# Reordering the head of a one-core transformer step: features begun on half of k, and two groups of additions moved to GpSimd

## What is computed

```python
mod = silu(c) @ w_mod + b_mod                       # nine vectors of 1024: shift, scale, gate x 3
h = rmsnorm(x, ng[0]) * (1 + sc1) + sh1
x = x + g1 * 0.5 * (silu(h @ w_gate) * (h @ w_up)) @ w_down      # FFN 1, 1024 -> 2816 -> 1024
h = rmsnorm(x, ng[1]) * (1 + sc2) + sh2
...                                                  # attention group and recurrent group, w_out
x = x + g3 * 0.5 * swiglu(rmsnorm(x, ng[2]) * (1 + sc3) + sh3)   # FFN 2
y = rmsnorm(x, final_g)
```

## Time and profile before

| | us |
|---|---|
| median of three runs | 2238.14 |
| the profiled execution | 2237.18 |
| its span in the trace | 2235.4 |
| PE busy | 2161.9 (97%) |
| DVE busy | 1537.1 (69%) |
| ACT busy | 825.0 (37%) |
| POOL busy | 67.6 (3%) |

### The profile page before, as it was taken

The page is one execution under the profiler, slowest core; times in us unless marked ns, Lnnn a source line. Parts: engine busy times, 40 slices in busy tenths (PEclk is TensorE's granted clock), DMA queues, the critical chain, the costliest instruction groups (busy, mean ns, idle before and its releaser), DMA issues.

```text
span 2235.4 us, 34069 instructions
## 1 busy us (share of the span) xinstructions
PE 2161.9 (97%) x13144; PEld 2100.3 (94%) x13144; DVE 1537.1 (69%) x2543; ACT 825.0 (37%) x1503; POOL 67.6 (3%) x120
## 2 busy tenths in 40 slices
PE   5999999999999999999999999999999999999997
PEld 4989999999999999899988889899999999999996
DVE  6977777777878865766767874695555547756556
ACT  5632232234212133565257762453222323411122
POOL 0000000000000000000023130000000000000000
PEclk9999999999999999999999999999999999999999
DMA  7333323334534403001133211132121223521312
GB/s 294 134 106 121 120 96 136 105 123 141 179 127 157 145 19 150 30 29 48 38 84 110 55 41 38 61 112 89 59 84 63 75 72 113 179 94 59 114 31 85
DMA packets 86133, 219.03 MB, mean 98 GB/s; under 512 B 10624, under 2 KB 38144, under 8 KB 86016
## 3 DMA queue, kind: packets, MB, share of 16 engines
q1 hardware_dynamic: 82176, 208.52, 27.4%
q0 software_dynamic: 3840, 8.92, 1.8%
HBM read 172.56 MB, written 35.92 MB: 93 GB/s over the span
## 4 chain that ended last, share of the span: by engine, by line
PE 87%; DVE 6%; ACT 3%; DMA 2%; issue 1%; SPq 0%; DVEq 0%; POOL 0%; ACTq 0%
PE ps L818 15%; PE ps L819 15%; PE ps L820 15%; PE ps L893 9%; PE ps L895 9%; PE ps L894 9%; PE ps L1073 7%; PE ps L1204 2%; PE ps L1149 1%; PE ps L1055 1%; PE ps L1190 1%; PE ps L1157 1%; DMA sb_stage<-in_w_mod 1%; ACT sb_pr L1721 1%; DVE sb_nmx L2461 1%
## 5 line engine op out<-in xcount | busy, mean ns | idle before, releaser
L818 PE MATMUL ps<-sb_hH,sb_wH 128*128 128x384 f32 x1664 | 563.0, 338 | 9.5 <-DVE sb_hL L1915 4.7
L819 PE MATMUL ps<-sb_hL,sb_wH 128*128 128x384 f32 x1664 | 557.2, 335 | 0.0
L820 PE MATMUL ps<-sb_hH,sb_wL 128*128 128x384 f32 x1664 | 557.2, 335 | 0.0
L818 PEld LDWEIGHTS ps<-sb_hH,sb_wH 128*128 128x128 f32 x1664 | 313.1, 188 | 16.9 <-DVE sb_hL L1915 5.4
L819 PEld LDWEIGHTS ps<-sb_hL,sb_wH 128*128 128x128 f32 x1664 | 313.4, 188 | 1.2 <-issue 0.3
L820 PEld LDWEIGHTS ps<-sb_hH,sb_wL 128*128 128x128 f32 x1664 | 313.3, 188 | 0.0
L2225 DVE SCALAR_TENSOR_TENSOR sb_x<-ps,sb_mod,sb_x 128x384 f32<-128x384 f32 (+2 forms) x384 | 186.1, 514 | 172.2 <-PE ps L820 167.0
L893 PE MATMUL ps<-sb_hH,sb_wH 128*128 128x384 f32 x704 | 236.2, 336 | 5.1 <-DVE sb_tmp L2085 3.9
L894 PE MATMUL ps<-sb_hL,sb_wH 128*128 128x384 f32 x704 | 235.9, 335 | 0.0
L895 PE MATMUL ps<-sb_hH,sb_wL 128*128 128x384 f32 x704 | 235.7, 335 | 0.0
L1368 ACT ACTIVATE sb_wH<-sb_wide 128x512 fp32r<-128x512 f32 x176 | 110.9, 633 | 228.7 <-DVE sb_wide L1969 223.7
(11 more groups left out here) (259 smaller groups left out, 3799.7 us busy)
## 6 DMA issues: line engine op xcount, KB each, us to landing
sb_raw<-in_w_gate SPq DMA_DIRECT2D x56, 512.0 KB, 3.6
sb_raw<-in_w_up SPq DMA_DIRECT2D x56, 512.0 KB, 3.5
sb_raw<-in_w_mod SPq DMA_DIRECT2D x56, 512.0 KB, 3.6
hidden<-sb_tmp SPq DMA_DIRECT2D x132, 192.0 KB, 2.1
sb_hid_raw<-hidden SPq DMA_DIRECT2D x40, 576.0 KB, 6.4
sb_raw<-in_w_dn SPq DMA_DIRECT2D x80, 256.0 KB, 2.6
sb_stage<-in_w_mod SPq DMA_DIRECT2D x4, 2048.0 KB, 15.7
sb_raw<-in_w_in SPq DMA_DIRECT2D x16, 512.0 KB, 3.5
```

The source lines that it names most:

```text
L818: pe.matmul(o, wH, xH, start=begin, stop=False)
L819: pe.matmul(o, wH, xL, start=False, stop=False)
L820: return pe.matmul(o, wL, xH, start=False, stop=end)
```

## The change

Five things change, all but the last two in the first 100 us:

1. **Transfers.** Three small tensors instead of ten are issued ahead of the `w_mod` blocks; the other seven come behind the second block. Weights of feature index 0 come between the second and the third block, weights of index 1 and 2 ahead of x of chunks 1 and 2.
2. **TensorE's order.** Features 0 and 1 are no longer run whole after the fourth `w_mod` block, but in parts (`early_part`) of k, around and between the products of the third and fourth block. ScalarE's and VectorE's orders in the head are rewritten to match (`early_one` splits one A block alone). `stats` and `spread` of chunks 1 and 2 move to features 2 and 3.
3. **Sums of chunk 2.** The seven additions of the squares of chunk 2 go from VectorE to GpSimd (`last_square`).
4. **Front differences.** The four differences of each `op_front`, 16 instructions in each of the two FFNs, go from VectorE to GpSimd (`op_differences`); casts and low parts wait for the last GpSimd instruction that reads their tile (`OP_LAST_READ`).
5. **A series.** The 16 small steps (and five more) for softplus of the recurrent part move from the head into the FFN's down stage (`series_step`).

The diff, cut to its core:

```diff
+OP_LAST_READ = {B11: 1, T3: 2, T1: 3, B22: 3, T2: 4, B21: 4, T4: 4}
...
+        SMALLS = ((cin[:], "c"), (bmod[:], "bmod"), (ng[:], "ng"))
+        LATER_SMALLS = ((glam[:, 0], "glam"), (fg[:], "fg"), (convw[:], "convw"), (convb[:], "convb"),
+                        (gbias[:], "gbias"), (h0[:], "h0"), (subg[:], "subg"))
...
         def mod_bank(n):
-            return 6 if n % 2 else 7
+            return 2 if n % 2 else 7
+        def early_bank(z, w, u):
+            return (2, 7)[u] if (z, w) == (0, 2) else 3 + u + 2 * (w % 2)
...
-            for b in MOD_FIRST:
+            for b in MOD_FIRST[:2]:
+                stage_load(b)
+            for dst, name in LATER_SMALLS:
+                sp.dma_start(dst, a[name]).then_inc(gw_in, 16)
+            early_load(0, 0)
+            for b in MOD_FIRST[2:]:
+                stage_load(b)
+            early_load(0, 1)
+            early_load(0, 2)
             x_load(1)
-            load_one(0, 0, 1, MAIN + 1)
-            load_one(0, 1, 1, MAIN + 1)
             x_load(2)
+            early_load(0, 3)
...
+            def last_square(k):                      # GpSimd
+                s, buf = nrm[0], sum_buf(0, 2)
+                n = square_at(0, 2, k)
+                pool.wait_ge(s["sq"], n + 1)
+                if k > 1:
+                    pool.wait_ge(s["acc"], added_at(0, 2, k - 1))
+                pool.tensor_tensor(buf, buf if k > 1 else tmp[:, (n - 1) % 2], tmp[:, n % 2], ALU.add).then_inc(s["acc"], 1)
+            def op_differences(z, p):                # GpSimd; the same four leave op_front on VectorE
+                base = 16 * z + 4 * p
+                pool.wait_ge(front, base + 4)
+                pool.tensor_tensor(op_raw(T1, p), op_raw(T3, p), op_raw(B11, p), ALU.subtract).then_inc(front_pool, 1)
...
+            for k in range(1, KT):
+                last_square(k)
+            for p in range(KT // 2):
+                op_differences(0, p)
...
-                             {(1, 0, 2): (stats, 1), (1, 1, 0): (spread, 1), (1, 1, 6): (stats, 2), (2, 0, 6): (spread, 2)})
+                             {(2, 0, 2): (stats, 1), (2, 1, 0): (spread, 1), (2, 1, 5): (stats, 2), (3, 0, 3): (spread, 2)})
...
+            early_part(0, 0, (0, 1))                 # TensorE, after two of four mod_products
+            mod_products(2)
+            early_part(0, 1, (0, 1))
+            for u in range(2):
+                early_part(0, u, (2, 3))
+            mod_products(3)
+            early_part(1, 0, range(4))
+            for k in (4, 5):
+                for u in range(2):
+                    early_part(0, u, (k,))
+            early_part(1, 1, range(4))
+            for k in (6, 7):
+                for u in range(2):
+                    early_part(0, u, (k,))
+            for u in range(2):
+                early_part(1, u, range(4, KT))
...
-            h_hi(0, 0, range(4))                     # ScalarE
-            early_cast(0, 0, 0)
+            h_hi(0, 0, (0,))
+            early_one(0, 0, A11)
+            h_hi(0, 0, (1,))
+            early_one(0, 0, A21)
...
+            squares(0, 2, x_in, range(3))
             root_copy(0, 1)
+            squares(0, 2, x_in, range(3, KT))
+            silu_first(0, 1, early_bank(0, 1, 0))
+            early_cast(0, 0, 3)
+            early_cast(0, 1, 3)
+            load_root()
             root_of(0, 2)
```

More of the change, by code:

```diff
@@ L810, in _ @@
                     sub_norm(c, hd)
+            for p in range(KT // 2):
+                op_differences(1, p)
         @blk.tensor
@@ L864, in _, with first_chunk @@
             stats(0, 0)
-            pe.wait_ge(c_ready, 1)
-            pe.wait_ge(smalls, N_SMALL)
+            pe.wait_ge(cons, 4)
             mod_products(0)
             spread(0, 0)
[L869 to L875, removed]
+            mod_products(1)
+            def first_chunk(z, u, n, w, between=None, index=0, ks=range(KT)):
+                bank = early_bank(z, index, u)
+                for k in ks:
                     o = ((A11, A12), (A21, A22))[u][k // 4]
@@ L965, in hooks @@
                     return between
-                for w in range(EARLY):
+                for w in range(0 if z else 2, EARLY):
                     for u in range(2):
-                        first_chunk(z, u, w + 1, FT * z + w - 1 if w > 1 else FT * z if z else None, hooks(w, u), w)
+                        first_chunk(z, u, w + 1, FT * z + w - 1 if w > 2 - z else FT * z if z else None, hooks(w, u), w)
                 feature(z, 0, 0, True, 28 * z)
@@ L1512, in ffn_act @@
             def ffn_act(z):
-                for w in range(0 if z else 1, EARLY):
-                    silu_first(z, FT * z + w, 3 + 2 * (w % 2))
+                for w in range(0 if z else 2, EARLY):
+                    silu_first(z, FT * z + w, early_bank(z, w, 0))
                     if w + 2 <= EARLY:
@@ L2305, in _, with low_at_tile @@
             scale_of(0, 0, 4)
-            apply(0, 0, None, range(0, 4))
-            dve.wait_ge(rl_exp, 1)
-            link(dve.tensor_scalar(q, y, 2.0, None, ALU.add))
-            link(dve.reciprocal(q, q))
-            link(dve.tensor_tensor(y, y, q, ALU.mult))
-            link(dve.tensor_tensor(q, y, y, ALU.mult))
-            link(dve.memset(r, 1.0 / 17))
-            for n in range(15, 0, -2):
-                link(dve.tensor_tensor(r, r, q, ALU.mult))
-                link(dve.tensor_scalar(r, r, 1.0 / n, None, ALU.add))
+            def low_at_tile(n, at):
+                return lambda k: early_one(0, n, at[k]) if k in at else None
+            apply(0, 0, low_at_tile(0, {1: A11, 2: A21}), range(0, 4))
             mod_add(2)
+            early_one(0, 0, A12)
+            early_one(0, 0, A22)
             mod_add(3)
@@ L2319, in _ @@
             scale_of(0, 4, KT)
-            shift_step(0)
-            early_low(0, 0, 0)
-            apply(0, 0, None, range(4, 6))
-            early_low(0, 1, 0)
-            apply(0, 0, None, range(6, KT))
-            early_low(0, 0, 1)
-            for k in range(1, KT):
-                sum_square(0, 1, k)
-            early_low(0, 1, 1)
-            inverse_of(0, 1)
-            for k in range(1, KT):
-                sum_square(0, 2, k)
-            early_low(0, 0, 2)
+            apply(0, 0, low_at_tile(1, {4: A11, 6: A21}), range(4, KT))
+            early_one(0, 1, A12)
+            early_one(0, 1, A22)
+            for k in range(1, 4):
+                sum_square(0, 1, k)
+            early_low(0, 0, 2)
+            for k in range(4, KT):
+                sum_square(0, 1, k)
+            early_low(0, 1, 2)
+            inverse_of(0, 1)
+            hid_first(0, 0)
+            shift_step(0)
+            hid_first(0, 1, early_bank(0, 1, 1))
+            early_low(0, 0, 3)
+            early_low(0, 1, 3)
             inverse_of(0, 2)
-            early_low(0, 1, 2)
             ffn_dve(0)
```

105 lines of the change are left out of this document (66 added, 39 removed).

## The result

| | before | after |
|---|---|---|
| median, six runs each | 2238.16 us | 2247.63 us |
| lowest to highest | 2234.83 to 2239.04 | 2245.70 to 2248.77 |
| span in the trace | 2235.4 us | 2243.9 us |

The ratio is 1.0045, with a 95% interval of 1.0034 to 1.0055: the changed kernel is slower by about 9.5 us. The prediction was 2236.1 us, its range ended at 2241.5, and "slower" had a chance of 0.13. It was wrong.

What follows compares the result with a forecast made beforehand. TensorE (PE), busy 2161.9 of 2235.4 us, was taken as the bound. 1.0 us from the head and 1.0 from the front differences made 2.0 us less, 2238.14 to 2236.1; range 2230.5 to 2241.5.

Steps and rivals of the forecast that it cites:

- The transfers and the start of the features: Head: blocks 1 and 3 land 1.4 us later, yet features 0 and 1 end 6.7 to 8.1 us earlier.
- GpSimd's additions: Sums of chunk 2: seven additions at 1.10 us each, spaced 1.22, ending at 66.0 instead of 62.0 us on VectorE.
- second case: TensorE behind its wait for `stats` 2: a slow stretch brings it to 71.1 us instead of 69.7.
- The second FFN: GpSimd's 19 us of differences lie beside four features of 8.3 us there: no effect on time.
- Gain left: 1.0 us: Head, at `spread` 2: it ends at 71.05 us, where TensorE reached the same matmul at 72.1 before; 1.0 us won.
- Front differences: First FFN: VectorE relieved of 8 us, GpSimd's 19 us just covered, 1.0 us won; lower end nothing.
- The wait at 111 us: TensorE's wait of 1.27 us at 111.53: gone or halved, 1.0 us of it won.
- GpSimd and VectorE hold each other: Rival, front differences: VectorE stands 17.6 us for GpSimd's 16 against 8 relieved, giving 2246 us; chance 0.11.
- its sign of being wrong: Sign for the blocking rival: VectorE's multiplications between 70 and 90 us much over 0.6 us apart.

Runs made afterwards that it cites:

- e6: Kernel before with only SP's order changed, stores of hidden tiles behind the weight loads: 2244.96 us (before 2238.36), ratio 1.0031.
- e1: Changed kernel with the front differences of both FFNs back on VectorE: 2248.11 us (before 2237.89), ratio 1.0041.
- e3: Changed kernel with stores ahead of loads in SP's queue and front differences back on VectorE: 2241.49 us (before 2237.89), ratio 1.0015.
- e8: e4 with VectorE's four front groups of the first FFN one feature later: 2238.98 us (before 2238.36), ratio 1.0005.
- e7: e2 with GpSimd's subtractions replaced by one-input multiplications by 1.0, front values not the reference's: 2237.94 us (before 2238.36), ratio 0.9997.
- e4: e3 with the sums of chunk 2 back on VectorE too: 2238.98 us (before 2237.89), ratio 0.9999.
- e10: Kernel before with only the seven additions of chunk 2's squares moved to GpSimd: 2243.29 us (before 2237.55), ratio 1.0022.
- e5: Kernel before with only the front differences of both FFNs moved to GpSimd: 2244.87 us (before 2238.36), ratio 1.0023.
- e2: Changed kernel with stores of hidden tiles ahead of the waiting weight loads in SP's queue: 2245.25 us (before 2237.89), ratio 1.0036.
- e11: e3 with four of the first FFN's 16 front differences on GpSimd, none of the second's: 2242.75 us (before 2237.55), ratio 1.0024.

## Why the prediction was wrong

**Right.** The transfers and the start of the features: block 3's products ended at 37.2 (predicted 37.8), features 0 and 1 at 52.1 (six matmuls of 0.173 before `stats` 1; predicted 52.3). GpSimd's additions: 1.00 us each at a spacing of 1.13 (1.10 and 1.22), TensorE's wait for them 4.99 us (5 to 6 was named), `spread` 2 at 70.61 (70.3). This last number is right by luck: the inverse that it was to wait for was ready at 69.0, and TensorE came at 70.6, because the first eleven matmuls behind its wait of 4.99 us ran at half clock, 1.6 us in all (the prediction had such a stretch for TensorE only as its second case). The second FFN cost nothing, although the contention is there too: in 1463 to 1500 us four low parts take 4.9 to 5.4 us, and TensorE works through. Before, then after:

```profile
1463.00:1500.00 37.00, 37.00 (x216) 37.00 (x215) 34.27 (x63) 22.17 (x45) 0.00 (x0) 1.00 0.33 111
```

```profile
1463.00:1500.00 37.00, 37.00 (x216) 37.00 (x215) 35.41 (x46) 15.87 (x30) 20.38 (x16) 1.00 0.39 122
```

**The step that was missing: the order of SP's queue.** The prediction costed when the head's weights land and never asked what stands behind a load that waits. The new order puts each store one feature's loads (gate and up) further back, behind loads that wait for the low parts VectorE makes after that store's own tile. Alone it costs 7.55 us by the landmark and 6.4 by the head mark (e6), and 7.1 and 6.8 in the new head with the differences on VectorE (e1 against e3). Neither the sum nor a rival had it.

**The failed step in the sum, "Gain left: 1.0 us".** It set the end of `spread` 2, 71.05, beside the time at which TensorE reached the same matmul before, 72.1, and took the difference as won. But TensorE's position is not what is waited for there. VectorE is: it is busy almost without a gap from the front's start to 110 us (before, 43.8 of the 47 us from 64 to 111), and its start is `spread` 2, which stood at 64.70. The comparison should have been of VectorE's first use of it, 66.07 before and 71.98 after. In e3 TensorE did have 0.8 us of that gain, and lost it to waits of 2.42 and 1.48 us, which follow VectorE's work (e8, e7). The sums on GpSimd cost 3.6 us in the new head (e3 against e4) and 5.1 alone (e10), about 1.6 and 2.7 of it as half clock behind TensorE's wait for them; the start on half of k gives some of it back. Against before the head with the sums is not 1.0 better but 2.2 worse (e3).

**The failed step "Front differences": 1.0 won, GpSimd's 19 us hidden.** GpSimd did finish (at 98.5 us instead of 92 to 95), and the price was on VectorE: -1.0 became +4.4 alone (e5) and +5.9 in the new head (e2 against e3). The wait at 111 us, forecast as gone or halved, was 3.88 us (at 118.59). The rival "GpSimd and VectorE hold each other" had the mechanism and its direction, and its sign of being wrong (multiplications of 1.37 us) came true, but it had 0.11. That its 2246 us lie near the measured time is luck: it had put all of the loss on the contention, which alone makes 4.4 us (e5). What I set against it was one row in which only GpSimd gave way; there GpSimd's instructions had one input. The rival was also mis-sized, at 1.1 us for each instruction with 8 us relieved; measured are 0.7 us on each low part beside one.

**How they add up.** By landmarks, alone: 4.4 + 7.55 + 5.1 = 17 us, less 1.35 for all the rest of the change together (e4; the transfers, the start on half of k and the series were not run apart); the measured total is 9.75. By head marks it is 4.7 + 6.4 + 3.9 = 15 us, less 1.3, against 8.9. One part of the overlap is the clock: e5 and e6 each hold the half clock behind a wait of 3.9 us near 111, 1.9 us by the head mark, and the changed kernel holds it once. For the rest my explanation is that VectorE idle for a late store can't also be slowed: on top of the late stores the differences cost 0.4 us (e1 against after), on top of the differences the late stores cost 1.6 (e2 against after). That is why undoing either one alone showed almost nothing.

**Open.** Why e4 with a landmark 1.35 us earlier has no lower median: both kernels spread over some 7 us between executions, with granted clocks from 0.990 to 0.995, and 1.35 us are too few to be told apart there. e4's three lowest of 12 runs (2233.93 to 2234.94) lie below the lowest of the 24 of before beside them (2235.53), but one of the first six of before took 2234.83. Nor was it tried to take the stores off SP's queue.

## What to carry to other kernels

When a queue's order changes, read for each entry what it may wait for, and then who waits for the entries behind it; a store that stands behind a load comes late by whatever that load waits for, and so does the engine that needs the buffer which the store empties. When a step is moved, measure its gain at the first reader on the engine that is busy without gaps, not at the engine that issues it. Before two-input work goes from VectorE to GpSimd, ask what VectorE will run beside it: where that was two-input work, the move cost time here (e5 against before, e2 and e11 against e3) and gained in no run; an eviction with one input in PSUM kept its 0.54 us (77.46 in after).

## What the runs showed of the hardware

- VectorE and GpSimd, each with two SBUF inputs: a VectorE multiplication of 384 columns takes 1.37 us instead of 0.61, four low parts of 512 columns 5.28 to 5.52 instead of 2.48, a GpSimd difference 1.46 instead of 1.00. Both lose. The Trainium skill ("SBUF — State Buffer", Who interferes with whom) has the rule that a VectorE instruction with two SBUF inputs contends with a GpSimd instruction that reads SBUF; the trace now agrees, for both engines.
- The same beside a GpSimd instruction with one input: 0.86 and 3.0 us. The Trainium skill makes no difference there between a GpSimd instruction with one input and one with two; in these runs it is the larger part of the price.
- The clock. After TensorE had waited 3.88 (after) or 3.96 us (e8) in one piece, the next matmul took 0.66 instead of 0.41 us and the ones behind it 0.52 instead of 0.33. The same came behind a wait of 4.99 us (after, at 65.11) and behind 3.02 and, six matmuls on, 1.11 us (e10). After a wait of 1.48 us it stayed at 2.4 GHz (e4), and after 2.42 too. Waits of 3.4 us went both ways: 0.41 at 132.07 before, 0.66 in e2, e5 and e10. The windows of after and of e4 behind the wait:

```profile
120.00:124.00 4.00, 4.00 (x14) 0.50 0.00 0
```

```profile
112.00:116.00 4.00, 4.00 (x25) 1.00 0.00 0
```

  So 3.9 us of waiting in two pieces cost e4 1.5 us less than e8 in one (landmarks 835.31 and 836.86). The clock of e4 fell once later, behind a wait of 1.93 us (0.63 granted in 124 to 128 us; before, behind 1.91 us, it did not fall), and there it cost nothing, since TensorE's next wait was 1.83 us instead of 3.4.
